# Gate rows in a two-layer diffusion block: built by TensorE products and ScalarE copies, or by two transfers through device memory

## The reference, cut to what matters

```python
ml = (jax.nn.silu(c) @ w_mod[i] + b_mod[i])[:, None, :]
mc = jax.nn.silu(c_ctx) @ w_mod[i] + b_mod[i]
sh1, sc1, gt1, sh2, sc2, gt2 = jnp.split(ml, 6, axis=-1)
csh1, csc1, cgt1, csh2, csc2, cgt2 = jnp.split(mc, 6, axis=-1)
...
xl = xl + gt1 * rms_norm(yl, g_mix_post[i])
fl = swiglu(rms_norm(xl, g_ffn_pre[i]) * (1.0 + sc2) + sh2, w_ffn_in[i], w_ffn_out[i])
xl = xl + gt2 * rms_norm(fl, g_ffn_post[i])
if need_ctx:
    xc = xc + cgt1 * rms_norm(yc, g_mix_post[i])
    ...
    xc = xc + cgt2 * rms_norm(fc, g_ffn_post[i])
```

## Time and profile before

| | us |
|---|---|
| median of 3 runs | 1823.67 |
| lowest and highest | 1821.22, 1824.87 |
| the profiled execution | 1823.63 |
| its span, first to last instruction | 1821.8 |
| PE busy | 1720.4 |
| ACT busy | 650.1 |
| POOL busy | 606.8 |
| DVE busy | 562.2 |
| moved by DMA | 204.03 MB |

### The profile page before, as it was taken

How to read it: one execution, slowest core, us unless ns; L and a number is a source line. 1 busy time by engine, 2 the same in 40 slices (tenths; PEclk the granted TensorE clock), 3 DMA queues, 4 the chain that set the end, 5 groups by cost and what they waited for, 6 DMA issues and landing times.

```text
span 1821.8 us, 26539 instructions
## 1 busy us (share of the span) xinstructions
PE 1720.4 (94%) x10634; PEld 1416.6 (78%) x10634; DVE 562.2 (31%) x1059; ACT 650.1 (36%) x1130; POOL 606.8 (33%) x436
## 2 busy tenths in 40 slices
PE   4899998999999999999999999998999799999997
PEld 1778886777877787777899878886887688788876
DVE  1324546616410011101766431003771511011103
ACT  3334124635522222221555343224772522213221
POOL 1221223027543433332400033332542344444443
PEclk8899998999999999999999999998999899999999
DMA  8543210013466236523656653433001133333331
GB/s 305 191 131 110 56 39 12 2 58 105 132 212 200 92 121 223 187 81 103 212 162 173 184 151 90 98 92 93 25 2 47 47 105 92 94 95 102 93 93 69
DMA packets 209429, 204.03 MB, mean 112 GB/s; under 512 B 16326, under 2 KB 180636, under 8 KB 209308
## 3 DMA queue, kind: packets, MB, share of 16 engines
q1 hardware_dynamic: 198504, 169.20, 30.8%
q10 hardware_dynamic: 10804, 33.14, 5.7%
HBM read 200.22 MB, written 2.10 MB: 111 GB/s over the span
## 4 chain that ended last, share of the span: by engine, by line
PE 86%; DVE 3%; ACT 3%; issue 3%; POOL 2%; DMA 1%; SPq 1%; ACTq 0%; DVEq 0%; POOLq 0%
PE ps L1560 43%; PE ps L1587 28%; PE ps L1733 3%; PE ps L1789 3%; PE ps L1754 3%; PE ps L1640 2%; POOL w_lo L497 2%; DMA mod_early<-in_w_mod 1%; ACT w_hi L798 1%; PE ps L1665 1%; PE ps L1801 1%; PE ps L1675 1%; PE ps L1922 1%; ACT prob L888 0%; ACT full L822 0%
## 5 line engine op out<-in xcount | busy, mean ns | idle before, releaser
L497 POOL TENSOR_TENSOR w_lo<-w_raw,w_hi 128x1024 fp32r<-128x1024 f32 (+1 forms) x201 | 480.1, 2391 | 992.1 <-ACT w_hi L798 991.9
L1560 PE MATMUL ps<-h_hi,w_hi 128*128 128x512 f32 (+1 forms) x1488 | 499.6, 354 | 14.5 <-DVE w_lo L497 7.1
L1560 PE MATMUL ps<-h_hi,w_lo 128*128 128x512 f32 (+1 forms) x1488 | 493.7, 350 | 0.0
L1560 PE MATMUL ps<-h_lo,w_hi 128*128 128x512 f32 (+1 forms) x1488 | 492.4, 349 | 0.0
L798 ACT ACTIVATE w_hi<-w_raw 128x1024 fp32r<-128x1024 f32 (+1 forms) x275 | 286.9, 1044 | 359.7 <-PE ps L1587 356.0
L1560 PEld LDWEIGHTS ps<-h_hi,w_hi 128*128 128x128 f32 x1488 | 271.7, 191 | 63.8 <-issue 23.4
L1560 PEld LDWEIGHTS ps<-h_hi,w_lo 128*128 128x128 f32 x1488 | 271.3, 190 | 36.6
L1560 PEld LDWEIGHTS ps<-h_lo,w_hi 128*128 128x128 f32 x1488 | 271.4, 190 | 35.6
L497 DVE TENSOR_TENSOR w_lo<-w_raw,w_hi 128x1024 fp32r<-128x1024 f32 x74 | 98.5, 1331 | 276.6 <-ACT w_hi L798 276.4
L1205 DVE TENSOR_TENSOR hid_f<-silu_g,ps 128x512 f32<-128x512 f32 (+1 forms) x66 | 39.4, 597 | 403.9 <-PE ps L1560 403.6
L1587 PE MATMUL ps<-w_hi,hid_hi 128*128 128x512 f32 x440 | 139.2, 398 | 7.6 <-DVE hid_lo L1210 2.4
(11 more groups left out here) (195 smaller groups left out, 1688.2 us busy)
## 6 DMA issues: line engine op xcount, KB each, us to landing
w_raw<-in_w_ffn_in SPq DMA_DIRECT2D x132, 512.0 KB, 3.9
w_raw<-in_w_ffn_out SPq DMA_DIRECT2D x66, 512.0 KB, 3.6
mod_raw<-in_w_mod ACTq DMA_DIRECT2D x47, 512.0 KB, 5.5
w_raw<-in_na_w_in SPq DMA_DIRECT2D x32, 512.0 KB, 3.7
mod_early<-in_w_mod SPq DMA_DIRECT2D x30, 512.0 KB, 9.5
w_raw<-in_ab_w_in SPq DMA_DIRECT2D x9, 512.0 KB, 4.5
mod_raw<-in_w_mod SPq DMA_DIRECT2D x9, 512.0 KB, 5.8
w_raw<-in_ab_w_in SPq DMA_DIRECT2D x16, 256.0 KB, 3.7
```

The costliest lines, as they stand in the source:

```text
L497: eng.tensor_tensor(w_lo[:, u % RING, 0:width], w_raw[:, u % RAW, 0:width], w_hi[:, u % RING, 0:width].bitcast(F32), ALU.subtract).then_in ...
L1560: mm = pe.matmul(o[0], sta(x, o), mov(y, o), start=first and n == 0, stop=last and n == 2)
```

## The change

The products and the copies go. In their place ACT stores gate_col's columns to a scratch in device memory, gate_rows (4 gates x 2 x 1024 floats), and later loads the row from there to all 128 partitions. gate_store(j) waits for the gate to be computed; gate_load(j) waits for the store, and for the end of the use of gate_b before (the first load for the last output of layer 0's recurrence). The stores and loads stand in ACT's program at these places: store 0 after the fifth unit of in0, load 0 ahead of attention(0); store 1 in the hook after the ninth step of the first fi0L half, ahead of that step's modulation loads, load 1 after its eleventh step; stores 2 and 3 at the end of fi0C; load 2 after the seventh unit of qk1; load 3 after the fifth step of layer 1's FFN. DVE waits for the load instead of the copies, for both rows of a gate at once.

```diff
+        gate_rows = nc.dram_tensor("gate_rows", (4, 2, D), F32).ap()
...
-        gb_base, gb_after = [0, 2, 4, 5], [0, 6, 12, 16]
-        gb_need = {"out0L": (1, 2), "out0C": (1, 2), "fo0L": (3, 4), "fo0C": (3, 4), "out1L": (5, 5), "fo1L": (6, 6)}
+        gb_after = [0, 6, 12, 16]
+        gb_need = {"out0L": 1, "out0C": 1, "fo0L": 2, "fo0C": 2, "out1L": 3, "fo1L": 4}
...
-            def gate_rows(b, n_lc):
-
-                for lc in range(n_lc):
-                    act.wait_ge(gb_ready, gb_base[b] + lc + 1)
-                    if gb_after[b]:
-                        act.wait_ge(post_n, gb_after[b])
-                    act.activation(gate_b[:, lc, :], ps(4 + 2 * lc, 0, D), ACT.Copy).then_inc(gb_done, 1)
+            def gate_store(j):
+                act.wait_ge(mod_der, 2 * j + 2)
+                n = 2 if j < 2 else 1
+                act.dma_start(gate_rows[j, 0:n].rearrange("v (k p) -> p v k", p=P), gate_col[:, j, 0:n],
+                              allow_slow_non_contiguous=True).then_inc(gate_out, 16)
+
+            def gate_load(j):
+                act.wait_ge(gate_out, (16, 32, 64, 64)[j])
+                if gb_after[j]:
+                    act.wait_ge(post_n, gb_after[j])
+                else:
+                    act.wait_ge(gl_o, NT)
+                rows, n = gate_rows[j], 2 if j < 2 else 1
+                act.dma_start(gate_b[:, 0:n], bass.AP(rows.tensor, rows.offset, [[0, P], [D, n], [1, D]]))\
+                    .then_inc(gate_in, 16)
...
+                if i == 4:
+                    gate_store(0)
+            gate_load(0)
             attention(0, lambda: None)
 
 
-            gate_rows(0, 2)
             feed(sp("out0C"))
...
-                    8: lambda: mod_copy(6), 10: lambda: mod_copy(7)})
+                    8: lambda: [mod_copy(6), gate_store(1)], 10: lambda: [mod_copy(7), gate_load(1)]})
             feed(sp(("fi0L", 1)) + RING - 1)
-            ffn_in(("fi0L", 1), FH, SEQ, {0: lambda: gate_rows(1, 2), 4: lambda: mod_copy(8), 7: lambda: mod_copy(9),
+            ffn_in(("fi0L", 1), FH, SEQ, {4: lambda: mod_copy(8), 7: lambda: mod_copy(9),
                                           9: lambda: mod_copy(10)})
...
             ffn_in("fi0C", FT, CTX, hooks)
+            gate_store(2)
+            gate_store(3)
             feed(sp("qk1") + 1)
...
+                    if i == 6:
+                        gate_load(2)
...
-            gate_rows(2, 1)
             def layer1_values(name, tiles):
...
-            ffn_in(("fi1L", 0), FH, SEQ, {4: lambda: gate_rows(3, 1)})
+            ffn_in(("fi1L", 0), FH, SEQ, {4: lambda: gate_load(3)})
...
-                dve.wait_ge(gb_done, gb_need[name][lc])
+                dve.wait_ge(gate_in, 16 * gb_need[name])
...
-            def gate_rows(j, n_lc):
-                pe.wait_ge(mod_der, 2 * j + 2)
-                for lc in range(n_lc):
-                    claim(4 + 2 * lc, 5 + 2 * lc)
-                    for k in range(KT):
-                        col = gate_col[:, j, lc, k:k + 1]
-                        mm = pe.matmul(ps(4 + 2 * lc, k * P, (k + 1) * P),
-                                       bass.AP(col.tensor, col.offset, [list(col.ap[0]), [0, P]]), ident[:],
-                                       start=True, stop=True)
-                    mm.then_inc(gb_ready, 1)
-                    read_by((4 + 2 * lc, 5 + 2 * lc), (gb_done, gb_base[j] + lc + 1))
```

More of the change, by code:

```diff
@@ L382, in build @@
         (mod_copied, mod_turned, mod_done, mod_der) = map(sem, ("mod_copied", "mod_turned", "mod_done", "mod_der"))
-        (gb_ready, gb_done) = map(sem, ("gb_ready", "gb_done"))
+        (gate_out, gate_in) = map(sem, ("gate_out", "gate_in"))
         (pre_ssq, pre_ms, pre_rs, pre_xs, pre_tr, pre_full, pre_hi, pre_lo) = map(sem, (
@@ L1984, in _ @@
                 read_by((2 * i, 2 * i + 1), (half_done, i + 1))
-            ffn_in(("fi0L", 1), FH, 0, SEQ, {0: lambda: gate_rows(1, 2), 1: lambda: modulation_columns(7),
+            ffn_in(("fi0L", 1), FH, 0, SEQ, {1: lambda: modulation_columns(7),
                                              5: lambda: modulation_columns(8), 8: lambda: modulation_columns(9),
@@ L2036, in _ @@
             pre_turn("ffn1L", range(1, LT))
-            ffn_in(("fi1L", 0), FH, 0, SEQ, {4: lambda: gate_rows(3, 1)}, "ffn1L")
+            ffn_in(("fi1L", 0), FH, 0, SEQ, None, "ffn1L")
             claim(*range(8))
```

## The result

The changed kernel takes 1832.32 us (median of four, 1831.39 to 1833.28), the kernel before 1822.53 in the same comparison. The ratio is 1.0052, 95% interval [1.0037, 1.0068]: slower by 9.8 us. The prediction was 1812.3, with 1810.5 to 1818.8 as its range: wrong in sign, by 20 us.

What follows compares the result with a forecast made beforehand. PE was taken to bound the kernel (busy 94% of the span, 86% of the chain). Gains of 4.20 + 3.49 + 1.93 + 1.70 = 11.32 us, with 0 for transfers, gave 1823.63 - 11.32 = 1812.3 us, range 1810.5 to 1818.8.

Steps and rivals of the forecast that it cites:

- The sum of the four gains: PE time saved at the four places of the removed products: 4.20 + 3.49 + 1.93 + 1.70 = 11.32 us.
- place 0: Before layer 0's first output projection: PE then waits only for DVE's last low part, starting at 376.78; 4.20 us gained.
- place 1: In layer 0's FFN: the copies were already hidden, so only PE's own time counts; 3.49 us gained.
- places 2 and 3: Before layer 1's values, PE waits for the last key copy, 1.93 us gained; in layer 1's FFN, 1.70 us.
- the clock rival: PE's 2.3 us idle before the output projection drops its clock to half rate, costing 4.8 us: 1817.1; chance 0.09.
- The price of a 4-byte run: Each run of a store costs its DMA engine 5 to 100 ns; middle near 50 ns, 6 us a store.
- my threshold of 45 ns: At store 1: a run may cost 45 ns (5.79 us of room) before PE stops at 579.68 for modulation loads.
- the first rival: Store 1 delays the modulation loads behind it; PE waits up to 7.0 us at 579.68: 1812.5 to 1819.3; chance 0.17.
- So I take 0: Added stores and loads cost PE nothing: 0 at store 1, with 7.0 us as other end; 0 for issue on ACT.
- whether their issue holds ACT: Rival: store issues hold ACT by their runs, about 10 us for 2048, delaying PE: 1819.6, or 1825 with runs; chance 0.09.
- What would show it: Signs in the after profile, including clock 1.00 at the projection; weight loads landing in much more than 3.9 us contradict it.
- The slow store as a rival: At 579.68 PE waits 128t - 5.8 us for t ns a write; over 0.2% slower from 162 ns; chance 0.08.

Runs made afterwards that it cites:

- turned kernel: The changed kernel with each gate turned by a PE product and stored in 512-byte runs at moved places, the last two sharing one store: 1811.47 us, ratio 0.9940.
- experiment 5: The kernel before, products and copies kept, plus the change's four 4-byte-run stores into a scratch nobody reads: 1843.15 us, ratio 1.0116.
- Experiment 7: As experiment 3, but store 3 issued 55 us after store 2, still in the second attention: 1810.34 us, ratio 0.9935.
- experiments 2 and 4: 2: the changed kernel with all stores in 32-byte runs, in an order making gates wrong, 1811.45 us, ratio 0.9933; 4: the turned kernel.
- experiment 3: The changed kernel with its 4-byte stores moved to supposedly quiet places, stores 2 and 3 together in the second attention: 1819.79 us, ratio 0.9992.

## Why the prediction was wrong, step by step

- **The sum of the four gains, 11.32 us: right in total, in part by luck.** Places 0 and 2 wait for what was named. In the turned kernel the three stretches are shorter than before by 2.4 (place 0: 4.20 less 1.6 for the clock), 3.2 (place 1: 3.49) and 5.8 us (places 2 and 3: 3.63, and 2 us more that I can't place). The clock's loss and those 2 us cancel. Those 2 us need not come from the change: experiment 5, which keeps all products, is 1.6 us shorter there too. Experiment 7 is 11.95 us under the kernel before, experiments 2 and 4 some 10, and experiment 5 less 11.3 gives the changed kernel within 0.5.
- **Place 0, 4.20 us: start right, clock wrong.** The start moved by 4.3 us. The argument against the clock rival was an idle stretch of the same 2.3 us at 427.5 that kept 1.00; here it fell, at 1.6 us, not the rival's 4.8. And that stretch keeps its clock in only two of eleven profiles; the kernel before happened to be one of them. One row of one place couldn't carry "granted clock 1.00".
- **The price of a 4-byte run: wrong in kind.** I took two rows whose runs are 512 bytes and more and drew a price for each run from them, 5 to 100 ns, with 50 as a middle. The store took 10.7 us (84 ns for each of an engine's 128 runs), inside those bounds, but with half the runs it takes 10.9, and its packets keep the engines busy for only some 1.3 us of it. By my threshold of 45 ns PE should then wait 10.7 less 5.8 to 6.6, 4 to 5 us, at the modulation rows; it waited 5.3 there, and lost some 3 more at half rate: 1.3 in the 24 matmuls of the rows (1.50 us in the earlier trace rows, 2.80 now) and 1.7 until 587. So the mechanism of the first rival was right, its chance of 0.17 too low, and its price left out the clock.
- **"So I take 0" for the transfers: the step that failed.** The sum has nothing for what the stores do to other transfers; they cost some 21 us, 8.2 at store 1 and 12.9 at stores 2 and 3. For store 1, between bounds far apart, with a threshold of 45 ns inside them, the value next to nothing wasn't the likeliest.
- **Stores 2 and 3: never priced, the larger half of the same step.** For them I asked only whether their issue holds ACT (it doesn't, 0.38 us, so that rival falls) and who waits for their rows (nobody). I did not ask what else was under way on the other queue. SP's weight loads of the second FFN product have less slack than they were late by, and two stores of 10.9 us on end stretched one to 19.3. This is 13 of the 21 us, and no rival held it; without it the changed kernel would stand near 1819.4, by subtraction. The last sentence of "What would show it", weight loads landing in much more than 3.9, named the sign without a price.
- **The slow store as a rival** (162 ns for each run, 1832.1 at 200) hits the time by chance: with its one wait at 579.68, it is not what happened.
- **The Trainium skill's rule** ("DMA: Bandwidth & Descriptors", Rules for kernel authors: a last dimension that isn't contiguous becomes one descriptor for each element, rearrange instead) pointed to the loss: experiments 2 and 4, which follow it, are 21 us faster than the changed kernel. Its count of descriptors agrees with the 2080 packets of q10 about stores 2 and 3 in experiment 3, but the time did not go by their number (10.7 and 10.9 us for 2048 and 1024). That page's read-modify-write below 512 bytes would charge runs of 64 bytes as well; these landed in 1.4 us.

## What to carry to other kernels

A transfer that nobody waits for still costs if another queue's loads have no slack: before adding one, price it by its landing, and look up what lands on every queue meanwhile. Turn a column into rows on the chip before it is stored, so that runs are long; where that can't be done, put such stores singly in stretches without close loads. Bounds drawn from rows of another kind give a range, not a middle to bet on.

## What the hardware showed that I had not expected

- A store of 8 KB in 4-byte runs takes 10.7 us, half of it 10.9, the same runs 64 bytes apart 5.3 and 512 bytes apart 4.4; 128 such runs take 7.5 us within 512 bytes and 1.4 when 1 KB apart.
- While such a store is under way, other loads wait as well, on its own queue and on another: 512 KB in 15.1 and 19.3 us in place of 4.8 and 3.6, and all of the core's transfers at 2 to 66 GB/s for 11 us.
- Beside two such stores on end ACT stood for 11.2 us, DVE for 7.3 and PE for 6.0, with no wait that the profile names and no instruction load under way; 55 us apart the stores cost nothing.
- The granted clock fell after 2.25 us without matmuls at 375 us in six profiles of six, and after 2.31 us at about 427 in nine of eleven: the same wait in the same code gives both. With products in the gap at 375 it stayed at 1.00.
